# Differential attention interleaved with its projections by head pairs

## Reference, cut to what matters

```python
q, k, v = split(h @ w_qkv, 3)            # h: 528 x 1024, w_qkv: 1024 x 3072
q = rope(q, 8 heads, 2 maps, 64) * 64**-0.5
k = rope(k, 8 heads, 2 maps, 64)
v = v.reshape(T, 8 heads, 128)
s = einsum('qhcd,khcd->hcqk', q, k)      # c: the two maps of a head
p = softmax(where(causal, s, -inf))
a = p[:, 0] - lam * p[:, 1]              # one matrix a head
o = rms_norm(a @ v, subln) * (1 - lambda_init)
y = o.reshape(T, 1024) @ w_o
```

## Time and profile before

| | |
|---|---|
| Runs | 2136.45 us median of 3 (2134.37 to 2136.66) |
| Profiled execution | 2127.97 us, span 2125.9 us |
| TensorE matmul busy | 1901.7 us, 89% of the span |
| VectorE, ScalarE, GpSimd busy | 1215.9, 637.3, 99.7 us |
| Mean granted TensorE clock | 0.945 |

### The profile page before, as it was taken

The page is one execution under the profiler, slowest core; times in us unless marked ns, Lnnn a source line. Parts: engine busy times, 40 slices in busy tenths (PEclk is TensorE's granted clock), DMA queues, the critical chain, the costliest instruction groups (busy, mean ns, idle before and its releaser), DMA issues.

```text
span 2125.9 us, 35032 instructions
## 1 busy us (share of the span) xinstructions
PE 1901.7 (89%) x14910; PEld 1634.2 (77%) x14910; DVE 1215.9 (57%) x2260; ACT 637.3 (30%) x1218; POOL 99.7 (5%) x53
## 2 busy tenths in 40 slices
PE   2999946997998777999999996987999999999997
PEld 1444435954997446999999996787866899999996
DVE  6004466414655664677775345798366477777423
ACT  1032321213212553322222231310377532222221
POOL 0000000100000000000000011232200000000000
PEclk7999967997999987999999998998999999999998
DMA  8220310010452000333333332143200132233331
GB/s 328 87 79 11 121 68 1 4 40 30 116 136 69 1 1 25 98 97 91 90 90 98 94 97 80 53 118 91 60 1 1 31 90 90 90 92 95 93 100 60
DMA packets 51146, 160.40 MB, mean 75 GB/s; under 512 B 8112, under 2 KB 9136, under 8 KB 50864
## 3 DMA queue, kind: packets, MB, share of 16 engines
q1 hardware_dynamic: 43504, 147.35, 22.4%
q10 hardware_dynamic: 7488, 10.82, 2.0%
HBM read 146.31 MB, written 2.10 MB: 70 GB/s over the span
## 4 chain that ended last, share of the span: by engine, by line
PE 79%; DVE 16%; issue 2%; ACT 1%; DMA 1%; ACTq 0%; SPq 0%; DVEq 0%
PE banks L469 17%; PE banks L470 17%; PE banks L471 16%; PE banks L1467 8%; PE banks L1623 3%; PE banks L1771 3%; PE banks L536 2%; DVE arena L1363 2%; DVE top L1362 2%; PE banks L514 1%; PE banks L590 1%; PE banks L526 1%; DVE stat L1126 1%; PE banks L750 1%; PE banks L562 1%
## 5 line engine op out<-in xcount | busy, mean ns | idle before, releaser
L469 PE MATMUL banks<-hn_hi,w_hi 128*128 128x264 f32 x2288 | 658.7, 288 | 30.3 <-DVE hn_lo L1042 14.2
L470 PE MATMUL banks<-hn_lo,w_hi 128*128 128x264 f32 x2288 | 654.0, 286 | 0.0
L471 PE MATMUL banks<-hn_hi,w_lo 128*128 128x264 f32 x2288 | 653.5, 286 | 0.0
L808 ACT ACTIVATE w_hi<-raw 128x1024 fp32r<-128x1024 f32 x207 | 219.4, 1061 | 897.5 <-PE banks L471 858.1
L469 PEld LDWEIGHTS banks<-hn_hi,w_hi 128*128 128x128 f32 x2288 | 436.5, 191 | 34.7 <-issue 20.3
L470 PEld LDWEIGHTS banks<-hn_lo,w_hi 128*128 128x128 f32 x2288 | 437.2, 191 | 0.1
L471 PEld LDWEIGHTS banks<-hn_hi,w_lo 128*128 128x128 f32 x2288 | 434.8, 190 | 0.0
L1036 DVE TENSOR_TENSOR w_lo<-raw,w_hi 128x1024 fp32r<-128x1024 f32 x181 | 221.5, 1224 | 199.5 <-ACT w_hi L808 199.4
L1467 PE MATMUL banks<-hn_raw,ring 128*128 128x512 f32 x416 | 186.2, 603 | 20.6 <-DVE hn_raw L2013 20.6
L469 PE MATMUL banks<-a_hi,w_hi 128*128 128x264 f32 x704 | 199.6, 284 | 1.6 <-DVE u_in L1249 1.6
L470 PE MATMUL banks<-a_lo,w_hi 128*128 128x264 f32 x704 | 200.5, 285 | 0.0
(11 more groups left out here) (337 smaller groups left out, 2627.3 us busy)
## 6 DMA issues: line engine op xcount, KB each, us to landing
raw<-in_weights SPq DMA_DIRECT2D x207, 512.0 KB, 3.6
ring<-in_weights SPq DMA_DIRECT2D x50, 512.0 KB, 6.0
arena<-arena ACTq DMA_DIRECT2D x144, 66.0 KB, 2.2
arena<-in_gate_w SPq DMA_DIRECT2D x8, 512.0 KB, 3.7
h<-in_xT SPq DMA_DIRECT2D x2, 1024.0 KB, 10.4
out_t<-h SPq DMA_DIRECT2D x4, 512.0 KB, 2.8
arena<-in_alibi SPq DMA_DIRECT2D x1, 1024.0 KB, 10.5
arena<-in_cosT ACTq DMA_DIRECT2D x2, 264.0 KB, 2.9
```

Of the source, the lines that this page charges most:

```text
L469: mm(o, w[0][:, j, :], x[0][:, k, t], start=first, stop=False)
L470: mm(o, w[0][:, j, :], x[1][:, k, t], start=False, stop=False)
L471: ins_ = mm(o, w[1][:, j, :], x[0][:, k, t], start=False, stop=last)
L808: nc.scalar.activation(w_hi[:, j % SPLIT, :], raw[:, j % RAW, :], ACT.Copy).then_inc(S["w_hi_done"], 1)
```

## The change

The 24 slots are put in a new order: four groups, each with two q slots, two k slots and two v slots of two heads. The first group is projected alone. In each of the next three groups TensorE does ten attention steps for the two heads of the group before, put at fixed k steps (`STEP_AT`). A step turns unit u, makes the scores of unit u + 1 and multiplies the values of unit u - 1. Units 30 to 39 follow the projections, with scores two to three units ahead. The first 31 units have their scores in banks 4 and 5 only, the projections use banks 0 to 3, and the value transposes go into the slot's own banks. VectorE reads each slot of a pair by itself (`da_first`, `da_second`), with the factor of q in the product in place of scaled tables. GpSimd makes all low halves from the fourth slot to the second slot of the output projection. The fifth tile's two maps stand in one pair of banks, on partitions 0 to 15 and 32 to 47: one reduce, one exponential, one scaling for both, a turn of 48 rows, and two products for each key tile, one a map, which are summed in PSUM.

```diff
+    def sc_at(u):
+        return 4 if u <= 30 else 2 * ((u - 31) % 3)
+    def da_slots(g):
+        return 2 * (g % 2)
+    STEP_AT = (6, 10, 14, 19, 23, 28, 32, 36, 41, 45)
-    POOL_SLOTS = range(S_DSA + 7, S_DSAO + 2)
+    POOL_DA = range(S_DA + 3, S_DAO + 2)
+    POOL_DSA = range(S_DSA + 7, S_DSAO + 2)
 # TensorE
+        def da_scores(u):
+            hd, n, w = UNITS[u]
+            if u <= 30:
+                pe.wait_ge(S["a_exp"], u)
+            elif u < 34:
+                pe.wait_ge(S["v_tok"], 8)
+                pe.wait_ge(S["a_exp"], 31)
+            else:
+                pe.wait_ge(S["a_exp"], u - 2)
+            if n == 0 and hd % 2 == 0:
+                for b in range(2):
+                    pe.wait_ge(scattered[b], 128 * (hd // 2 + 1))
...
+                for a in range(2):
+                    for c in range(2):
+                        r = slice(64 * c, 64 * c + 64)
+                        mm(psum[32 * c:32 * c + 16, b + a, 0:HALF], qs[r, hd, n * P:n * P + w], kz[r, hd, a * HALF:(a + 1) * HALF], start=True, stop=a == 0)
...
+        def da_values(u):
...
+                    mm(out_bank(n), pt[0:kj, u % 2, j * 48:j * 48 + 16], v, start=j == 0, stop=False)
+                    last = mm(out_bank(n), pt[0:kj, u % 2, j * 48 + 32:j * 48 + 48], v, start=False, stop=j == n)
...
+        def da_step(u):
+            da_turn(u)
+            da_scores(u + 1)
+            if u:
+                da_values(u - 1)
+        def da_free(g):
+            group, r = divmod(g - 2, 6)
+            if g >= 2 and r < 4:
+                pe.wait_ge(S["rope_read"], 4 * group + r + 1)
+            elif g >= 2:
+                pe.wait_ge(S["v_tok"], 2 * group + r - 3)
+        def da_project():
+            for g in range(N_DA):
+                group, r = divmod(g, 6)
+                w = slot(S_DA + g)
+                da_free(g)
+                for k in range(KT):
...
+                    last = both(g, w, (hn_hi, hn_lo), k, k, k == 0, k == KT - 1, at=da_slots(g))
+                    if k == KT - 1:
+                        last.then_inc(S["slot_used"], 1)
+                    if k == 3 and r == 5:
+                        da_v_transpose(2 * group)
+                    if k == 3 and r == 0 and group:
+                        da_v_transpose(2 * group - 1)
+                    if g == 6 and k == 4:
+                        da_scores(0)
+                    if group and 8 * r + k in STEP_AT:
+                        da_step(10 * (group - 1) + STEP_AT.index(8 * r + k))
...
+            da_turn(30)
+            da_scores(31)
+            da_scores(32)
+            da_scores(33)
+            da_values(29)
+            for u in range(31, 40):
...
 # ScalarE, t = u % 10
+                if u < 30:
+                    da_copy(u)
+                    da_exps(u + 1)
+                    if t in (0, 2, 4, 5, 7, 9):
+                        ahead(S_DA + 6 * group + (0, 2, 4, 5, 7, 9).index(t))
+                    if t == 3:
+                        scatter(2 * group, group, to_plain_q)
+                    elif t == 6:
+                        scatter(2 * group + 1, group, to_k)
 # VectorE: combine(u), soft(u + 1), output copies, then
+            def with_projections(group, t):
+                g = 6 * group
+                if t == 0:
+                    da_first(2 * group, g)
+                elif t == 2:
+                    da_second(2 * group, g + 1)
+                elif t == 3:
+                    da_rotated(2 * group)
+                elif t == 4:
+                    da_first(2 * group + 1, g + 2)
+                elif t == 5:
+                    da_second(2 * group + 1, g + 3)
+                elif t == 6:
+                    da_rotated(2 * group + 1)
+                elif t == 7:
+                    da_value_rows(2 * group, g + 4)
+                elif t == 8:
+                    da_tokens(2 * group)
+                elif t == 9:
+                    da_value_rows(2 * group + 1, g + 5)
 # GpSimd
+        for n in POOL_DA:
+            weight_rest(n)
 # layout on the host
-        _groups(_rope_split(qkv[:, :1024], 16)), _groups(_rope_split(qkv[:, 1024:2048], 16)), _groups(qkv[:, 2048:]),
+        by_head_pair(_groups(_rope_split(qkv[:, :1024], 16)), _groups(_rope_split(qkv[:, 1024:2048], 16)), _groups(qkv[:, 2048:])),
```

More of the change, by code:

```diff
@@ L557, in pair_scores @@
                 for c in range(2):
                     r = slice(64 * c, 64 * c + 64)
[L559 to L565, removed]
-                for c in range(2):
[L567 to L571, removed]
+                    mm(psum[:, b + c, 0:keys(n)], qs[r, hd, n * P:n * P + w], kz[r, hd, 0:keys(n)], start=True, stop=False)
@@ L972, in to_k @@
             return kz[:, m // 2, :]
[L974 to L983 removed]
+        ahead(S_DA)
+        norm_root(2)
+        ahead(S_DA + 1)
+        ahead(S_DA + 2)
+        scatter(0, 0, to_plain_q)
+        ahead(S_DA + 3)
+        ahead(S_DA + 4)
+        scatter(1, 0, to_k)
+        ahead(S_DA + 5)
         da_attention()
@@ new lines, in da_second, with da_rotated @@
+        def da_second(i, g):
+            ve.wait_ge(S["slot_used"], S_DA + g + 1)
+            for j, table in ((1, sin2), (3, cos2)):
+                if i % 2 == 0:
+                    last = V.scalar_tensor_tensor(out=halves(rope_t(i, j)), in0=da_pair(g), scalar=-0.125, in1=table, op0=ALU.mult, op1=ALU.mult)
+                else:
+                    last = V.tensor_tensor(halves(rope_t(i, j)), da_pair(g), table, ALU.mult)
+            last.then_inc(S["rope_read"], 1)
+        def da_rotated(i):
+            ve.wait_ge(S["rope_read"], 2 * i + 2)
+            V.tensor_tensor(rope_t(i, 0), rope_t(i, 0), rope_t(i, 1), ALU.subtract)
+            V.tensor_tensor(rope_t(i, 3), rope_t(i, 3), rope_t(i, 2), ALU.add).then_inc(S["rope_done"], 1)
@@ L1117, in da_attention, with da_first_group @@
+        def da_first_group():
+            st.did(V.memset(esum, 1.0))
+            st.did(V.memset(clast[0:32], 1.0))
+            st.did(V.tensor_copy(clast[32:64], nlam[32:64]))
+            st.link(V.memset(otok[:, 4, :], 0.0))
+            for i in range(2):
+                da_first(i, 2 * i)
+                da_second(i, 2 * i + 1)
+                da_rotated(i)
+            da_value_rows(0, 4)
+            da_tokens(0)
+            da_value_rows(1, 5)
         def da_attention():
-            for b in range(2):
-                ve.wait_ge(scattered[b], 128 * 4)
@@ L1120, in da_attention @@
-            st.did(V.memset(esum, 1.0))
-            st.link(V.memset(otok[:, 4, :], 0.0))
             def soft(u):
@@ L1292, in vector_block2 @@
         scale_tables()
[L1293 to L1298 removed]
+        da_first_group()
         da_attention()
@@ L2322, in mixed_up, with by_head_pair @@
         return w.reshape(D, 2, FT, P).transpose(0, 2, 1, 3).reshape(D, 2 * FFN)
+    def by_head_pair(q, k, v):
+        return np.concatenate([part[2 * i:2 * i + 2] for i in range(4) for part in (q, k, v)], axis=0)
     streams = [
```

300 lines of the change are left out of this document (169 added, 131 removed).

## The result

The changed kernel takes 2148.80 us (median of 6 runs, 2144.86 to 2150.49), the kernel before 2135.41 (6 runs, 2127.67 to 2137.16). The ratio is 1.0059, 95% interval 1.0045 to 1.0074: slower, by 12.6 us (9.6 to 15.8). A later measurement beside other kernels gave 1.0067 (1.0049 to 1.0085).

A forecast was written before the change was run, and what follows sets the result against it. TensorE was taken as the bound of the projections, with idle parts in the attention to fill. Up to the turn of unit 30 +6.5, clock +4, tail +5.1 gave +15.6 us on 2136.45: 2152.0 us, range 2130 to 2167.

The forecast's parts named there:

- step 1: Step 1 of groups 2 and 3, behind the first slot: the turn waits 2.1 us for VectorE's combine.
- step 6: Step 6 of each group, behind the fourth slot: the turn waits 3.6 us for VectorE's combine, beside GpSimd's low half.
- The waits: TensorE's waits inside the three groups: 24.6 us with the first scores' start, about 14.4 without the exclusion.
- step 8: Step 8 of each group: eight scatter transfers stand ahead of ScalarE's copy and exponentials; the turn waits 1.3 us.
- the restart's 4.2: After slot 23, last value rows, transpose, token copies and the combine of unit 30 stand in line: 4.2 us.
- TensorE's work: Three groups of six slots with two heads, 60.4 us each: 179.3 us up to the turn of unit 30.
- The clock: Clock losses after six TensorE idles of 2 us or more: 0 to 9.6 us, taken as +4.
- Slot 2: In group 0, slot 2 waits for VectorE to read slot 0, starting at about 544.3 instead of 540.2.
- The tail: Heads 6 and 7: doubled products +3.9, scores 31 to 33 no longer ahead +2.2, fifth tile -1; net +5.1 us.
- TensorE is never kept waiting: Rival: the chains fit under the k steps everywhere; -13 us, 2123 us; chance 0.17.
- the exclusion does not bite: Rival: GpSimd's part falls between combines, 10.2 us fewer waits, 2 us fewer of clock; +3.4, 2140 us; chance 0.15.
- the two maps serialise in one bank: Rival's half, fifth tile's scores: 7.9 us; with 9.6 for half clock after every wait +29.1, 2166 us; chance 0.18.

The follow-up runs named there:

- run 1: The changed kernel with GpSimd filling the low halves of differential attention with zeros instead of computing them; ratio to the kernel before 1.0005.
- run 5: The changed kernel with the low halves back on VectorE, each right behind the combine that follows its slot; ratio to the kernel before 1.0013.
- run 2: The changed kernel with rope products, rotation and scatter one step later in VectorE's queue, behind the next combine; ratio to the kernel before 0.9967.
- run 9: The changed kernel with products with zeros on TensorE ahead of the waiting turns at steps 6 and 1; ratio to the kernel before 1.0073.
- run 10: The changed kernel with rope products behind the next combine and the fifth tile's second value product left out; ratio to the kernel before 0.9922.
- run 3: The changed kernel with the second map's value product of the fifth tile left out; ratio to the kernel before 1.0014.
- run 6: The changed kernel with the fifth tile's maps summed in the turn by a 48 x 16 matrix, one value product per key tile; ratio to before 1.0055, again 1.0041.
- run 7: The kernel before with the fifth tile's change alone, old order, low halves on VectorE; ratio to the kernel before 1.0023.

## Why the prediction was right, and where its terms were off

**The sign and the cause held.** Forecast +15.6, measured +12.6 (9.6 to 15.8); 2152.0 us against 2148.8. The change made TensorE wait for the combine, because projection work stands ahead of it in VectorE's queue and GpSimd's subtraction shuts out its first operation. Runs 1 and 5 take away GpSimd's reads, and with them the waits at step 1, half of those at step 6 and some 10 us or a little more; run 2 takes away both links, and with them both waits and 20 us. The Trainium skill (SBUF — State Buffer, Who interferes with whom) says that a VectorE instruction with two SBUF inputs contends with a GpSimd instruction that reads SBUF and not with one that only writes it. The traces agree on both halves: 2.06 us beside the subtraction, 0.22 beside the zero fill.

**The waits.** Forecast 3.6, 2.1 and 1.3 us for steps 6, 1 and 8; measured 3.38, 1.95 and 0.47 to 1.61 (step 8: 0.47, 1.61 and 0.47). Step 5 waited 1.25 and 1.02 us in groups 2 and 3, where the forecast had at most 0.9. TensorE's idle time from slot 2 to unit 30 is 24.2 us, forecast 28.8 (24.6 and the restart's 4.2, of which 2.40 + 0.80 came). Without the exclusion the forecast was 18.6 (14.4 and 4.2); run 1, from its slot 2 at 545.54 to 768.05, is busy 206.2 of 222.5 us, so idle 16.3. Groups of 70.8 and 71.4 us: at the upper edge of the 66 to 71.

**TensorE's work.** Forecast 203.1 us for this stretch (23.8 for the end of group 0, 179.3 for three groups), measured 205.8 in run 2, of which 2.7 are the clock behind slot 2, and 204.8 in run 9 with 1.6 of that kind. Without these both leave 203.1 to 203.2: this term was right. The fifth tile's values are 20 records in 2.38 us, forecast 2.60. For eight heads the forecast's 10.4 us compares with 9.6 by the ratios of runs 2 and 10.

**The clock: the term that was too small.** I took +4 of a range of 0 to 9.6. Busy time is 212.7 against my 203.1, and the work was right, so the clock cost 9.6 us: 1.7 behind slot 2's wait and some 8 behind the steps. That this is the upper end of my range is partly luck. I had counted 1.6 us behind each of six idles; the fall at 613 to 621 us cost 3.4, the next three 1.7 each, and behind the wait at 652.34 there was none. (These four sum up what the clock lacked of 1.00, 8.5 us with what fell into idle time.) I had also reasoned that a slower TensorE shortens the waits behind it. By run 9 it hardly does: its idle time of 10.65 us and the 14.0 us of waits that it filled make 24.7, against 24.2 with the falls. Single waits go both ways (step 8: 1.09, 1.08 and 1.09 us in run 9, against 0.47, 1.61 and 0.47).

**Slot 2.** It began at 546.18 against 544.3. My terms for it add up to 543.8, half a microsecond less than I wrote. VectorE's tables were ready at 543.1 instead of 541.1, and profiles of kernels that are alike up to there have slot 2 between 543.3 and 547.9 us, so this 1.9 is the scatter of single executions more than a term.

Together: 780.3 forecast with the clock term, +1.9 for slot 2, +5.6 for the clock, -4.6 for the waits, which is 783.2; measured 783.09.

**The tail: forecast +5.1, in the profiles +9.7.** Timeline of TensorE in the changed kernel at its start:

```profile
783.49 1.23 PE L580 MATMUL banks<-arena 64*128 64x256 f32 x4
...
784.98 1.65 PE L580 MATMUL banks<-arena 64*128 64x384 f32 x4
...
786.89 1.90 PE L580 MATMUL banks<-arena 64*128 64x512 f32 x4
...
794.08 0.33 PE L601 MATMUL banks<-ident,arena 128*128 128x128 f32 x1 [1.58 <-DVE arena L1269]
```

The turn of unit 31 comes 11.0 us behind that of unit 30, before 4.25 (774.10 less 769.85). The scores of units 31 to 33, which stood ahead of the turn of unit 30, now stand behind it and take 5.4 us, at half clock at first; I had priced that move at 2.2. From there on the tails differ by 2.9 us. In run 9, with the clock up, the tail is 61.4. The three doubled products, forecast at +3.9, measured 5.1 (run 3, 60.66 against 65.72) and 3.2 (run 10). How the rest of the 9.7 divides between order and clock was not separated further.

**Why the total was still near.** By the two profiles the sum is 7 us too small (+15.6 against +22.5). By the ratio it is 3 too large. Both are the same kernels: the medians lie 13.4 us apart, the profiled execution of before was 7.4 under its median and that of the changed kernel 1.7 over its own. Clock and tail were mis-sized in the profiles that they were read from, and the measured median hides it. That the total came within 3 us is therefore partly luck.

**The rivals.** That TensorE is never kept waiting fell with the first view; run 2, which comes near to it with 11.0 us of idle time, gives -7 us, where this rival said -13. That the exclusion does not bite fell with L1267's 2.06 us; run 1, which makes it come true, gives +1 (-2 to +4), where this rival said +3.4. That the two maps serialise in one bank fell with 385 ns in both kernels, and eight of these matmuls take 1.07 us in both (769.93 in the changed kernel, 711.63 in the earlier trace rows). The Trainium skill (TensorEngine Tiling (Array Packing), Gotcha 1) says that different row tiles cannot access one PSUM bank simultaneously; here they did, on partitions 0 to 15 and 32 to 47 of the bank, with the overlap and the duration of before. The other half of that rival, 9.6 us for the clock, came true in its size, though not with every wait followed by a fall.

## What to carry to other kernels

Before moving work to GpSimd, look in VectorE's queue for operations with two SBUF inputs on the path that sets the end, however small: one of 0.22 us became 2.06, and putting the large reads of PSUM behind the urgent chain instead of ahead of it gave back 20 us, with GpSimd as it was. In this kernel 14.0 us of waits of 2 to 3.4 us cost 7 to 8 us more for the clock behind them, about half as much again, while waits of 1.5 us (run 1) cost nothing more; a single wait can come without a fall. Take the clock of a profile's stage into account before two profiles are subtracted: the ratios of many runs said 13 us where two profiles said 23.

## What was not expected of the hardware

- Behind the three 3.38 us waits and one of the two 1.95 us waits the granted clock fell to 0.50 at the same places in two executions (613 to 621, 685 to 691, 723 to 727 and 757 to 763 us, within 1 us), though not behind each such wait in run 6. Filling the wait with useless products kept it at 1.00.
- GpSimd's zero fill of a 128 x 1024 tile (0.95 us) left VectorE's two-input operations at 0.22 and 0.48 us; its subtraction of that size (2.34 to 2.40 us) did not.
- Turning the fifth tile with products by a 48 x 16 fp32 matrix comes as two records for each key tile and takes 1.14 us, where the five transposes of the same tiles take about 0.4.
- One kernel's profiled executions differ by more than its ratio's interval: run 7's profile has its output projection 13 us later than before, its ratio says 5 us. Between 680 and 770 us its clock is 0.83, against 0.94 before.
